# Bidirectional encoder block with 64 routed experts: where VectorE and ScalarE read the registers of the next items

## What is computed

```python
def route(xf, w_router, router_bias):
    scores = jax.nn.sigmoid(xf @ w_router)
    ...
    return eidx, w                                   # 8 experts and gates for each token

def routed_experts(xf, eidx, gates, w_gate, w_up, w_down):
    # assignments sorted by expert, each expert's rows in blocks of 128
    def step(y, blk):
        tok, gate, e = blk
        xb = x_pad[tok]
        h = jax.nn.silu(xb @ w_gate[e]) * (xb @ w_up[e])
        out = (h @ w_down[e]) * gate[:, None]
        return y.at[tok].add(out), None
```

## Time and profile before

| | us |
|---|---|
| median of 3 runs (lowest, highest) | 1374.81 (1374.38, 1375.08) |
| profiled execution, its own time | 1372.31 |
| its span | 1370.6 |
| PE busy | 1313.6 (96% of the span) |
| DVE busy | 871.4 (64%) |
| ACT busy | 740.9 (54%) |
| POOL busy | 467.8 (34%) |
| mean granted TensorE clock | 0.988 of full speed |

### The profile page before, as it was taken

One profiled execution on the slowest core, in us unless ns is written; L12 is line 12 of the kernel. 1 busy time (PEld: TensorE's weight loads), 2 busy tenths in 40 slices (PEclk: granted clock), 3 DMA queues, 4 the chain that ended last, 5 costly groups with the idle time before them and its releaser, 6 DMA issues.

```text
span 1370.6 us, 26812 instructions
## 1 busy us (share of the span) xinstructions
PE 1313.6 (96%) x6031; PEld 1030.5 (75%) x6032; DVE 871.4 (64%) x1333; ACT 740.9 (54%) x1044; POOL 467.8 (34%) x608
## 2 busy tenths in 40 slices
PE   6999988999999999999999999999999999999996
PEld 5885465888545788888888887888888888778875
DVE  5430544355585677767776777767776777767767
ACT  5320244211002577677775766777766777676762
POOL 2431201000002344444443444444444444433463
PEclk9999999999899999999999999999999999999998
DMA  9604032011046799999999999999999999999988
GB/s 343 192 11 165 0 122 93 31 47 46 9 185 219 236 328 342 300 313 310 329 321 324 306 306 339 310 321 325 344 316 321 317 335 322 287 317 311 338 249 235
DMA packets 88307, 338.03 MB, mean 247 GB/s; under 512 B 12496, under 2 KB 23760, under 8 KB 71504
## 3 DMA queue, kind: packets, MB, share of 16 engines
q1 hardware_dynamic: 60912, 251.58, 47.7%
q0 software_dynamic: 27360, 86.01, 26.3%
HBM read 288.99 MB, written 65.27 MB: 258 GB/s over the span
## 4 chain that ended last, share of the span: by engine, by line
PE 87%; issue 4%; DVE 3%; DVEq 2%; ACT 2%; ACTq 1%; DMA 1%; POOL 0%; POOLq 0%; SPq 0%
PE ps L739 33%; PE ps_out L753 16%; PE ps L624 7%; PE ps L490 7%; PE ps L473 6%; PE ps L659 4%; PE ps L526 4%; PE ps L575 2%; DVEq L321 2%; PE ps L761 1%; PE ps L795 1%; PE ps_out L641 1%; PE ps L669 1%; DVE w_gu L1213 1%; PE ps_out L669 1%
## 5 line engine op out<-in xcount | busy, mean ns | idle before, releaser
L739 PE MATMUL ps<-w_gu,xTh 128*128 x1488 | 468.2, 396 | 15.1 <-DVE xTl L1384 10.6
L1213 DVE TENSOR_TENSOR w_gu<-raw_gu,w_gu (+1 forms) x256 | 296.7, 1220 | 68.5 <-ACT w_gu L969 68.5
L739 PEld LDWEIGHTS ps<-w_gu,xTh 128*128 128x128 f32 x1488 | 273.0, 188 | 73.5 <-issue 20.9
L739 PE MATMUL ps<-w_gu,xTl 128*128 x744 | 291.2, 391 | 0.0
L969 ACT ACTIVATE w_gu<-raw_gu (+1 forms) x256 | 249.7, 1058 | 0.1
L753 PE MATMUL ps_out<-w_dn,hTh 128*128 x744 | 242.0, 406 | 1.6 <-ACT ob L990 1.6
L1602 POOL DMA_INDIRECT y_rows_dram<-ob,idxs x90 | 146.8, 1631 | 143.1 <-ACT ob L990 124.8
L1220 DVE TENSOR_TENSOR w_dn<-raw_dn,w_dn (+1 forms) x128 | 151.4, 1223 | 21.4 <-ACT w_dn L973 20.9
L739 PEld LDWEIGHTS ps<-w_gu,xTl 128*128 128x128 f32 x744 | 139.7, 188 | 29.1
L753 PEld LDWEIGHTS ps_out<-w_dn,hTh 128*128 128x128 f32 x744 | 133.2, 189 | 26.9 <-issue 1.9
L753 PE MATMUL ps_out<-w_dn,hTl 128*128 x372 | 146.1, 393 | 0.0
(11 more groups left out here) (248 smaller groups left out, 1629.2 us busy)
## 6 DMA issues: line engine op xcount, KB each, us to landing
raw_gu<-in_w_gate SPq DMA_DIRECT2D x64, 1024.0 KB
raw_gu<-in_w_up SPq DMA_DIRECT2D x64, 1024.0 KB
raw_dn<-in_w_down SPq DMA_DIRECT2D x64, 1024.0 KB
y_rows_dram<-zero SPq DMA_DIRECT2D x1, 4608.0 KB, 20.0
x_ring<-in_x SPq DMA_DIRECT2D x8, 512.0 KB, 4.6
w_in_sb<-in_w_in SPq DMA_DIRECT2D x8, 512.0 KB, 10.1
xh<-in_x SPq DMA_DIRECT2D x8, 512.0 KB, 7.1
w_out_sb<-in_w_out SPq DMA_DIRECT2D x1, 4096.0 KB, 12.8
```

Of the source, the lines that this page charges most:

```text
L739: mm = pe.matmul(ps[3][:, :], x_[:, k, :], w_gu[:, bass.ds(at, 1), part, :, k, :], start=(k == 0 and part == 0 and x_ is xTh), stop=(k == ...
L1213: dv.tensor_tensor(gu_part(w_gu[:, :, 1, :, :, :], at, m), gu_part(raw_gu, at, m), gu_part(w_gu[:, :, 0, :, :, :], at, m).bitcast(F32), AL ...
```

## The change

On VectorE and ScalarE no register of an expert is read at the loop's jump any more. Each item reads for itself: "now" behind the gated rows hh and xT (on ScalarE behind xTh), where the item isn't given it by the item two before it in the same turn, and "ahead" right in front of the branch that uses it, behind hTl (VectorE) or ob (ScalarE). The third item of a turn gets its "now" from the first one. A turn makes five reads on each of the two engines, before and after. TensorE, GpSimd and SyncE read as before, and nothing is computed differently. The helper functions are unchanged.

```diff
--- before.py
+++ after.py
@@ -1003,38 +1003,38 @@
             def item(i, u, turn, now, coming, final=False):
 
                 silu(i)
-                if final:
-                    if u + 1 < TURN:
-                        evac_xT(i + 1)
+                if final and u == TURN - 1:
                     evac_h(i)
                     evac_out(i - 1, (u - 1) % TURN, turn)
-                    if u + 1 < TURN:
-                        for flag, e, at in (now, coming):
-                            with act.If(flag > 0):
-                                act.wait_ge(s_rd, e + 1)
-                                split_dn(at)
-                    return coming
-                ahead = expert(i + 2)
+                    return None
                 evac_xT(i + 1)
                 if isinstance(i, int) and i == 0:
                     act.wait_ge(s_yst[0], 16 * 4)
-
-                if not (isinstance(i, int) and i == 0):
-                    with act.If(now[0] > 0):
-                        act.wait_ge(s_rd, now[1] + 1)
-                        split_dn(now[2])
+                else:
+                    now = now or expert(i)
+                    if not final:
+                        with act.If(now[0] > 0):
+                            act.wait_ge(s_rd, now[1] + 1)
+                            split_dn(now[2])
                 evac_h(i)
                 if not (isinstance(i, int) and i == 0):
                     evac_out(i - 1, (u - 1) % TURN, turn if u else turn - 1)
+                if final:
+                    for flag, e, at in (now, coming):
+                        with act.If(flag > 0):
+                            act.wait_ge(s_rd, e + 1)
+                            split_dn(at)
+                    return None
+                ahead = expert(i + 2)
                 with act.If(ahead[0] > 0):
                     act.wait_ge(s_rg, ahead[1] + 1)
                     split_gu(ahead[2], range(GU_PARTS))
                 return ahead
 
             def turn_of_items(turn, final=False):
-                now, coming = expert(turn * TURN), expert(turn * TURN + 1)
-                for u in range(TURN):
-                    now, coming = coming, item(turn * TURN + u, u, turn, now, coming, final and u > 0)
+                third = item(turn * TURN, 0, turn, None, None)
+                item(turn * TURN + 1, 1, turn, None, third, final)
+                item(turn * TURN + 2, 2, turn, third, None, final)
 
             act.wait_ge(s_rg, 1)
             split_gu(1, range(GU_PARTS))
@@ -1398,37 +1398,35 @@
             def item(i, u, now, coming, final=False):
 
                 gated_h(i, u)
-                if final:
-                    if u + 1 < TURN:
-                        rest_xT(i + 1)
-                        with dv.If(now[0] > 0):
-                            rest_dn(now[2], now[1])
+                if final and u == TURN - 1:
                     rest_h(i)
-                    if u + 1 < TURN:
-                        with dv.If(coming[0] > 0):
-                            rest_dn(coming[2], coming[1])
-                    return coming
-                ahead = expert(i + 2)
+                    return None
                 rest_xT(i + 1)
                 if isinstance(i, int) and i == 0:
                     y0(NC - 1)
                     rest_h(i)
+                    coming = expert(i + 1)
                     dv.wait_ge(s_yst[1], 16 * 4)
                     with dv.If(coming[0] > 0):
                         rest_gu(coming[2], coming[1], range(GU_PARTS))
                 else:
+                    now = now or expert(i)
                     with dv.If(now[0] > 0):
                         rest_dn(now[2], now[1])
-                if not (isinstance(i, int) and i == 0):
                     rest_h(i)
+                if final:
+                    with dv.If(coming[0] > 0):
+                        rest_dn(coming[2], coming[1])
+                    return None
+                ahead = expert(i + 2)
                 with dv.If(ahead[0] > 0):
                     rest_gu(ahead[2], ahead[1], range(GU_PARTS))
                 return ahead
 
             def turn_of_items(turn, final=False):
-                now, coming = expert(turn * TURN), expert(turn * TURN + 1)
-                for u in range(TURN):
-                    now, coming = coming, item(turn * TURN + u, u, now, coming, final and u > 0)
+                third = item(turn * TURN, 0, None, None)
+                item(turn * TURN + 1, 1, None, third, final)
+                item(turn * TURN + 2, 2, third, None, final)
 
             def y0(c):
                 dv.wait_ge(s_sdn, c + 1)
```

## The result

| | before | after |
|---|---|---|
| median (lowest, highest), 4 runs each on one chip | 1374.60 (1373.83, 1375.08) | 1354.14 (1352.91, 1355.03) |
| ratio after / before, 95% interval | | 0.985 (0.983 to 0.987) |
| profiled execution, its own time | 1372.31 | 1355.03 |
| its span | 1370.6 | 1353.3 |
| PE busy | 1313.6 (96%) | 1310.0 (97%) |

The changed kernel is faster by 1.5%, 20.5 us. The forecast of 1355.1 us is 1.0 above the median. Its sign and its range held.

What follows compares the result with a forecast made beforehand. TensorE's chain bounds the kernel, losing 20.4 us at loop jumps to reads in VectorE's queue. -20.4 + 0.65 = -19.75 from 1372.31 gives 1352.6, plus 2.50 to the median: 1355.1 us; range 1353.6 to 1358, to 1361 with ScalarE's read eating slack.

Steps and rivals of the forecast that it cites:

- The loss at the jumps: VectorE's queue at the loop's jump: moving three reads away ends all 22 losses, -20.4 us.
- No cover at all: VectorE's third read, between hh and xTl: nothing hides it once the jump with two reads has made hh late.
- rival 5: VectorE at the jump: the jump itself, not the reads, delays hh; gain 7 us smaller, 1362; chance 0.03.
- The first turn: Item 0 on VectorE: "ahead" now read behind the wait for y0's stores, without cover, +0.65 us (0 to 0.72).
- VectorE's new places: "now" behind xTl and "ahead" behind hTl on VectorE: price 0.
- ScalarE's "ahead": Read between ob and w_gu on ScalarE: cover 0.61 us against cost 0.62, taken as 0, upper end 0.1 each.
- ScalarE's "now": Read behind xTh on ScalarE: w_dn some 0.15 us later, taken as 0; upper end 1 us over some 20 items.
- rival 2: ScalarE's reads in front of w_gu take twice 0.28 us, costing 16.5 us in all: 1371.6; chance 0.02.
- rival 3: Long reads move along to ScalarE's w_gu, 1.12 us each, giving back 48 us: 1403, slower than before; chance 0.02.
- rival 1: ScalarE's "ahead" read partly eats the slack: 6.1 us per 0.1 us past it over 61 splits, 1361; chance 0.10.
- Rival 4: DMA engines become the bound in the expert loop; holding the pace to halfway gives 1365; chance 0.03.
- the floor of about 600 ns: Register reads at the skill page's stated minimum length would put the sum about 16 us higher, near 1371.

Runs made afterwards that it cites:

- one of the experiments: The changed kernel with one more VectorE read in front of "ahead", behind hTl; measured 1355.76 us, ratio 0.987.
- the experiment above: The changed kernel with one more ScalarE read in front of "ahead", between ob and w_gu; measured 1374.17 us, ratio 1.000.
- changed again: The changed kernel run again without any edit, beside three others on the same chip; measured 1352.79 us, ratio 0.985, profiled execution 1352.74.

## Why the prediction was right

**The loss at the jumps, -20.4.** Right: 20.3 in the profile, from 22 losses to none. The cause was also right, reads in VectorE's queue; undoing VectorE's part brings all of it back, undoing ScalarE's none. "No cover at all" for the third read was roughly so: it loses its cover only because the first two are ahead of it. That the jump by itself costs nothing (rival 5) shows in every jump of the changed kernel.

**The first turn, +0.65.** Right: items 0 and 1 took 22.45 us instead of 21.83, 0.62 more, and the idle time of 3.57 became 4.20.

**VectorE's new places, 0.** Right, and with room: a second read there cost at most 0.07 us in any item but the one that was held up by its down weights.

**ScalarE's "ahead", 0.** Right, and as near the edge as the sum had it. The cover of 0.61 and the cost of 0.62 were each good to some hundredths: w_gu began 5.29 to 5.33 us into its item (5.29 before), in three items 5.37 to 5.40, and the items behind these were 9.43 or 9.44 long. One more read passed through with 0.56 of its 0.62.

**ScalarE's "now", 0.** Right in the main: where ScalarE reads for itself w_dn comes some 2.20 us into its item instead of 2.05, the 0.15 forecast, and hTh at most 0.06 later, but in five items w_dn comes over 0.2 and hTh 0.10 to 0.13 later. Three of these five are the ones whose w_gu came at 5.37 to 5.40: the upper end of this term showed there, at 0.06 us an item.

**The sum.** -19.75 was forecast for the profiled execution, 1352.6. The first profile took 1355.03, 2.4 above it for the time before the loop; the second took 1352.74. The medians fell by 20.5 us (20.7 from the 1374.81 of the prediction): the step from the profiled execution to the median, +2.5, treated as fixed what is scatter. For the changed kernel it was -0.9 the first time (1354.14 less 1355.03) and +0.05 the second (1352.79 less 1352.74). So the parts inside the loop came out by their mechanism, but that the forecast lies within 1.0 us of the median is in part luck; it is 2.3 above the second median.

**The rivals.** 1 to 3 did not happen. Their prices were wrong, though, in one term: "times 61". When ScalarE's reads really were too long, 33 splits of the 61 paid. By my estimate from that run rival 2 would have ended near 1364 (33 times 0.27 is 8.9) and rival 3 near 1381 (33 times 0.79 is 26), still slower than before. The range, which rival 1 set, would have been a little narrower. Rival 3's premise, that long reads might move to where the split is, did not hold: reads late in an item stayed at 0.28. Rival 4 fell: the DMA engines carry the loop at 0.97 to 1.00 from 554 us on, and no engine waits for weights in it; one late w_dn in one of the experiments is all that shows of it. As for the floor of about 600 ns that the Trainium skill's page DMA: Bandwidth & Descriptors (Latency and other measured facts) states for a register load from a tensor: by it the changed kernel would have paid for its read in front of w_gu already, much as it paid for a second one in the experiment above. Its reads took 273 ns at the least, 280 in the median on ScalarE, and the measurement decides:

```profile
L321 ACTq TENSOR_LOAD <-tab x153: 273/280/1334, 413.8 to 1304.2; - x153
...
L321 DVEq TENSOR_LOAD <-tab x153: 300/308/653, 450.9 to 1305.3; - x153
```

## What to carry to other kernels

Count the register work that stands in a queue between two instructions of which the later one is waited for, and set it against the time in which the engine still works on what was handed over before: each read is free until the sum exceeds that cover, and then costs in full, so that the same read can be worth nothing or half the gain, by what stands ahead of it. Put reads behind the urgent instruction, or in front of one that waits for another engine anyway. And when a delay recurs in neighbouring items, don't multiply it by their number: the bottleneck's own stall gives the next item part of its slack back.

## What was not expected

**Which reads are long.** The two kinds of jump have one cause, and I had read only half of it. Of the 88 items from the fourth on, 27 split no w_dn (they are the second or a later item of an expert). In the kernel before, every one of these 27 has a read of over 0.5 us on VectorE's queue in its first 1.5 us, and none of the other 61 has; on ScalarE it is 25 and none. Ten of the 22 jumps that lost fall on such an item, those with the larger losses. With one read put back at the jump, seven jumps had a read of 0.72 to 0.90, all on such items. In the changed kernel, where these items read later, behind xTl or hTl, only one of the 27 has a long read, and the longest of VectorE's from 600 us on is 653 ns:

```profile
L321 DVEq TENSOR_LOAD <-tab x125: 300/307/653, 601.7 to 1298.3; - x125
```

The same stretch of the kernel before:

```profile
L321 DVEq TENSOR_LOAD <-tab x120: 299/311/1044, 608.6 to 1292.9; - x120
```

So what makes a read long is its moment at the start of such an item. The long reads also share their end. Here are those of one such item (from 579.08 us) in the kernel before, on ScalarE's, TensorE's and VectorE's queues:

```profile
L321 ACTq TENSOR_LOAD <-tab x1: 1076/1076/1076, 579.4 to 579.4; - x1
L321 PEldq TENSOR_LOAD <-tab x1: 1034/1034/1034, 579.4 to 579.4; - x1
...
L321 DVEq TENSOR_LOAD <-tab x1: 645/645/645, 579.8 to 579.8; - x1
```

VectorE's starts 0.4 us later and is 0.4 us shorter, so all three end at about 580.4. Of the 27 long reads on VectorE in the kernel before, 26 end between 1.31 and 1.51 us into their item, and of ScalarE's 25, 21 end between 1.23 and 1.41. The reads thus seem to wait for something that is over by then, on every queue. What that is wasn't tried and stays open.

**Scatter before the loop.** The first transpose of item 0, up to which no instruction differs, came at 443.3 us (before), 445.7 (changed) and 443.5 (changed again), and between 443.4 and 445.6 in the others. From 220 to 300 us the granted clock differs a little, before and after:

```profile
220.00:300.00 80.00, 73.66 (x353) 60.30 (x352) 32.46 (x75) 22.92 (x35) 7.18 (x17) 0.96 0.17 66
```

```profile
220.00:300.00 80.00, 73.67 (x351) 60.30 (x350) 32.48 (x74) 21.98 (x34) 6.52 (x16) 0.94 0.17 66
```

But the second profile of the changed kernel has 0.94 there too, and began its loop 2.2 us earlier, so this is a small part at most. The rest comes in steps at several places: against the second profile the first is 1.1 us behind by 42 us, 1.7 by 190 and 2.0 by 250. It wasn't followed further.
